# Griffin layer at full precision: six weight panels taken as F32R products of high and low parts, the first normalisation moved behind the products

## What is computed

```
h = rms_norm(x, mix_norm[0])
u = h @ w_in                                  # 1024 -> 2048
gate_branch, x_branch = split(u, 2)
gate_branch = gelu(gate_branch)
xc = causal_depthwise_conv(x_branch, conv_w, conv_b)       # width 4
r = sigmoid(blockwise(xc, w_r) + b_r); i = sigmoid(blockwise(xc, w_i) + b_i)
log_a = 8 * r * log_sigmoid(lam);  a = exp(log_a)
bt = sqrt(-expm1(2 * log_a)) * (i * xc)
h_t = a_t * h_(t-1) + bt_t                    # scan over the 256 tokens
x = x + (gate_branch * h) @ w_out             # 1024 -> 1024
```

## Time and profile before

| | |
|---|---|
| median of 3 runs | 1862.44 us (1861.78 to 1862.58) |
| the profiled execution | 1862.93 us |
| its span, first to last instruction | 1861.7 us |
| PE busy, share of the span | 1739.2 us, 93% |
| DVE, ACT busy | 779.5 us (42%), 584.5 us (31%) |
| mean granted clock of TensorE | 0.983 |
| end of the Griffin layer's last product | 110.8 us from the span's start |

### The profile page before, as it was taken

The page is one execution under the profiler, slowest core; times in us unless marked ns, Lnnn a source line. Parts: engine busy times, 40 slices in busy tenths (PEclk is TensorE's granted clock), DMA queues, the critical chain, the costliest instruction groups (busy, mean ns, idle before and its releaser), DMA issues.

```text
span 1861.7 us, 24238 instructions
## 1 busy us (share of the span) xinstructions
PE 1739.2 (93%) x9217; PEld 1037.3 (56%) x9218; DVE 779.5 (42%) x1132; ACT 584.5 (31%) x758; POOL 30.9 (2%) x56
## 2 busy tenths in 40 slices
PE   6999999988999999998999999999999998999995
PEld 6779997777999898887333332333323232333332
DVE  3544446754444547877322222322222212222224
ACT  1534555544445546653111111211112111111111
POOL 0000001000000020000000000000000000000000
PEclk9999999999999999999899999999999998999998
DMA  7355555421555553347699999999999996999995
GB/s 261 136 181 181 181 182 175 159 74 46 181 181 183 179 186 109 119 148 288 245 431 428 428 428 428 428 428 428 428 429 428 429 398 269 407 428 429 428 428 217
DMA packets 87186, 537.21 MB, mean 289 GB/s; under 512 B 10864, under 2 KB 10968, under 8 KB 62552
## 3 DMA queue, kind: packets, MB, share of 16 engines
q1 hardware_dynamic: 79088, 531.64, 70.9%
q10 hardware_dynamic: 8040, 4.73, 0.9%
HBM read 535.31 MB, written 1.05 MB: 288 GB/s over the span
## 4 chain that ended last, share of the span: by engine, by line
PE 63%; DMA 26%; DVE 6%; ACT 2%; issue 2%; ACTq 0%; SPq 0%; PEldq 0%; POOL 0%; DVEq 0%; POOLq 0%
DMA expert_ring<-in_expert_w_up 26%; PE psA L1951 19%; PE psA L537 12%; PE psB L497 11%; PE psB L520 4%; PE psB L389 3%; PE psA L520 2%; PE psB L508 2%; PE psA L412 1%; DVE w_low L478 1%; PE psA L1957 1%; PE psB L344 1%; PE psB L1339 1%; PE psB L1980 1%; PE psA L984 1%
## 5 line engine op out<-in xcount | busy, mean ns | idle before, releaser
L1951 PE MATMUL psA<-expert_ring,gathered_T 128*64 128x512 f32 x1024 | 456.5, 598 | 31.6 <-DMA expert_ring<-in_expert_w_up 31.6
L1952 PE MATMUL psA<-expert_ring,gathered_T 128*64 128x512 f32 x1024 | 456.5, 598 | 0.0
L478 DVE TENSOR_TENSOR w_low<-panel_ring,w_high 128x1024 fp32r<-128x1024 f32 x220 | 267.4, 1223 | 200.8 <-ACT w_high L471 200.0
L1951 PEld LDWEIGHTS psA<-expert_ring,gathered_T 128*64 128x64 f32 x1024 | 135.1, 137 | 346.6 <-issue 282.1
L471 ACT ACTIVATE w_high<-panel_ring 128x1024 fp32r<-128x1024 f32 x220 | 230.2, 1056 | 268.5 <-PE psA L537 105.5
L1951 PE MATMUL psA<-expert_ring,activated_T 128*64 128x512 f32 x528 | 240.5, 598 | 3.1 <-ACT activated_T L2209 0.9
L1952 PE MATMUL psA<-expert_ring,activated_T 128*64 128x512 f32 x528 | 240.5, 598 | 0.0
L2367 DVE TENSOR_SCALAR normed<-psA 128x512 f32<-128x512 f32 x32 | 22.1, 692 | 394.5 <-PE psA L1952 394.5
L2168 ACT ACTIVATE normed<-normed 128x512 f32<-128x512 f32 x32 | 20.2, 630 | 476.0 <-DVE normed L2367 476.0
L497 PE MATMUL psB<-hT_high,w_high 128*128 128x256 f32 x592 | 167.8, 283 | 0.0
L497 PE MATMUL psB<-hT_low,w_high 128*128 128x256 f32 x592 | 167.5, 283 | 0.0
(11 more groups left out here) (439 smaller groups left out, 2563.6 us busy)
## 6 DMA issues: line engine op xcount, KB each, us to landing
expert_ring<-in_expert_w_up SPq DMA_DIRECT2D x128, 2048.0 KB, 25.4
expert_ring<-in_expert_w_down SPq DMA_DIRECT2D x64, 2048.0 KB, 22.3
panel_ring<-in_mlp_w SPq DMA_DIRECT2D x32, 2048.0 KB, 7.9
panel_ring<-in_w_in SPq DMA_DIRECT2D x11, 2048.0 KB, 8.1
panel_ring<-in_fox_w_in SPq DMA_DIRECT2D x6, 2048.0 KB, 8.1
panel_ring<-in_lru_w_in SPq DMA_DIRECT2D x4, 2048.0 KB, 17.9
panel_ring<-in_lru_w_out SPq DMA_DIRECT2D x2, 2048.0 KB, 8.0
panel_ring<-in_fox_w_out SPq DMA_DIRECT2D x2, 2048.0 KB, 8.3
```

The lines of the kernel that those rows point to most:

```text
L478: V.tensor_tensor(w[1], view, w[0].bitcast(F32), ALU.subtract).then_inc(s.w_low, 1)
L1951: M.matmul(ps[0:SLOTS], lhsT, rhs[0], **flags)
L1952: return M.matmul(ps[SLOTS:P], lhsT, rhs[1], **flags)
```

## The change

The Griffin layer's panels go the way of all the others, and the queues of that layer are written anew.

- Panels 0 to 5 become parts 0 to 23: `high` on ACT, `low` on DVE, three F32R products on PE. `part_of` counts from panel 0.
- x is loaded by SP ahead of everything, each half with its own semaphore. The first panel comes as two halves, six of the small loads are issued by SP between them, and the four loads of the gate weights by SP after panel 1. ACT issues six small loads, after one Sqrt on a scratch tile.
- Raw x is transposed as it lands; only the gains (32 columns) are needed by then. 1/rms is made beside the first products, spread over all partitions by two matmuls with a diagonal (`r_diag`, `r_all`), and multiplied into the products as they are evicted (`pad`, `scale_gate`).
- The convolution goes by pairs of channel groups: ACT does the first tap (`first_tap`), DVE the other three (`taps`).
- The gates use Tanh of half the argument in place of Sigmoid, and c4 times the result plus c4 inside Tanh and Exp (per 128-channel group) in place of a multiplication on DVE. a squared is made on ACT. The polynomial for log_sigmoid(lam) goes from DVE to POOL.
- The gated hidden state is split into high and low as well (`gated_high`, `gated_low`).
- After the Griffin layer only counts in waits change.

```diff
 def weights_sp(k, g):
-    S.wait_ge(s.x_loaded, 16 * TT)
-    S.wait_ge(s.small, 16 * SMALL_LOADS)
+    for tt in range(TT):
+        S.dma_start(k.x[:, tt, :], a["x"][0, tt * P:(tt + 1) * P, :]).then_inc(s.x_loaded[tt], 16)
+    S.dma_start(k.panel(0, KD)[:, :, half[0]], sources[0][0][:, :, half[0]]).then_inc(s.first_half, 16)
+    small_loads_sp(k)
+    S.dma_start(k.panel(0, KD)[:, :, half[1]], sources[0][0][:, :, half[1]]).then_inc(s.panel_in[0], 16)
...
+        if p == 1:
+            griffin_loads_sp(k, g)
 def griffin_pe(k, g):
-    project_T(k, GRIFFIN, k.psB[0])
-    project_T(k, GRIFFIN + 1, k.psB[1])
-    gates(0)
-    M.wait_ge(s.evicted, 1)
-    project_T(k, GRIFFIN + 2, k.psB[0])
-    gates(1)
...
+    gains_pe(k)
+    for tt in range(TT):
+        x_T_pe(k, 0, tt)
+    M.wait_ge(s.h_low, 1)
+    product_T_tile(k, p, 0, up(0, 0), 0)
+    product_T_tile(k, p, 1, up(0, 1), 0)
+    M.wait_ge(s.h_low, 2)
+    product_T_tile(k, p, 0, up(0, 0), 1)
+    product_T_tile(k, p, 1, up(0, 1), 1)
+    columns_pe(k)
+    product_T(k, p, 2, up(0, 2))
+    M.wait_ge(s.r_spread, 2)
+    for tt in range(TT):
+        last = M.matmul(k.psA[:, 0, tt * P:(tt + 1) * P], k.ones[:], g.r_diag[:, tt, :], start=True, stop=True)
+    last.then_inc(s.r_rows, 1)
+    product_T(k, p, 3, up(0, 3))
+    for i in range(4):
+        product_T(k, p + 1, i, up(1, i))
+    gates(0)
+    M.wait_ge(s.padded, 2)
+    for i in range(4):
+        if i == 2:
+            gates(1)
+        product_T(k, p + 2, i, up(2, i))
+    M.wait_ge(s.padded, 4)
+    for i in range(4):
+        product_T(k, p + 3, i, up(3, i))
...
+    M.wait_ge(s.gated_low, 1)
+    for i in range(4):
+        product_out(k, p + 4, i, row(i), i == 0)
+    M.wait_ge(s.gated_low, 2)
+    product_out_tiles(k, p + 5, lambda i: row(4 + i), False, True, {(1, 0): lambda: x_T_pe(k, 1, 0)})
 def griffin_act(k, g):
+    def half_tanh(j, n):
+        A.wait_ge(s.gate_products, 2 * j + n + 1)
...
+            last = A.activation((g.ra, g.ib)[n][:, c, :], (g.r_ps, g.i_ps)[n][:, t, :], ACT.Tanh, scale=0.5,
+                                bias=g.half_b[:, KD * n + c:KD * n + c + 1])
+    def decay(j):
+        for f, to in ((ACT.Tanh, g.th), (ACT.Exp, g.ra)):
+            for c in range(4 * j, 4 * j + 4):
+                last = A.activation(to[:, c, :], g.ra[:, c, :], f, scale=g.c4[:, c:c + 1], bias=g.c4[:, c:c + 1])
...
+    squares_act(k, 0)
+    high_h(k, 0, 0)
+    highs(0, 1)
+    high_h(k, 0, 1)
+    highs(1, 3)
+    root_act(k, 0)
+    highs(3, 4)
+    A.wait_ge(s.cols_ready, 2)
+    A.activation(u, k.col("lam", KD), ACT.Abs).then_inc(*act.step())
+    A.activation(u, u, ACT.Exp, scale=-1.0).then_inc(s.lam, 1)
+    highs(4, 6)
+    first_tap(0)
+    highs(6, 8)
+    first_tap(1)
+    highs(8, 9)
+    first_tap(2)
+    highs(9, 11)
+    first_tap(3)
+    highs(11, 12)
+    half_tanh(0, 0)
+    decay(0)
+    half_tanh(0, 1)
+    highs(12, 13)
+    squares(0)
+    highs(13, 14)
+    root(0)
+    half_tanh(1, 0)
+    highs(14, 15)
+    decay(1)
+    highs(15, 16)
+    half_tanh(1, 1)
+    gelu(0)
+    highs(16, 17)
+    gated_high(0)
+    highs(17, 18)
+    squares(1)
+    highs(18, 19)
+    root(1)
+    highs(19, 20)
+    gelu(1)
+    highs(20, 21)
+    gated_high(1)
+    highs(21, 24)
 def griffin_dve(k, g):
+    gains_dve(k)
+    for tt in range(TT):
+        hT_dve(k, 0, tt, gain)
+    low_h(k, 0, 0)
+    lows(0, 1)
+    low_h(k, 0, 1)
+    lows(1, 2)
+    mean_square_dve(k, 0)
+    lows(2, 3)
+    root_dve(k, 0)
...
+    lows(3, 4)
+    columns_dve(k)
...
+    lows(4, 5)
+    V.wait_ge(s.r_rows, 1)
+    V.tensor_copy(g.r_all[:], k.psA[:, 0, 0:T]).then_inc(*dve.step())
+    pad(0)
+    lows(5, 6)
+    taps(0, 1, 2)
+    lows(6, 7)
+    pad(1)
+    taps(0, 3)
+    lows(7, 8)
+    taps(1, 1, 2)
+    lows(8, 9)
+    taps(1, 3)
+    pad(2)
+    lows(9, 10)
+    taps(2, 1, 2)
+    pad(3)
+    lows(10, 11)
+    taps(2, 3)
+    taps(3, 1, 2, 3)
+    lows(11, 12)
+    inputs(0)
+    lows(12, 13)
+    square_gap(0)
+    lows(13, 14)
+    scaled_inputs(0)
+    scan(0)
+    lows(14, 15)
+    scale_gate(0)
+    lows(15, 16)
+    inputs(1)
+    lows(16, 17)
+    gated(0)
+    gated_low(0)
+    lows(17, 18)
+    square_gap(1)
+    lows(18, 19)
+    scale_gate(1)
+    scaled_inputs(1)
+    lows(19, 20)
+    scan(1)
+    lows(20, 21)
+    gated(1)
+    gated_low(1)
+    lows(21, 24)
```

More of the change, by code:

```diff
@@ L604, in __init__ @@
     def __init__(self, k, c):
-        sb = lambda n, shape: k.sb(n, shape, ctx=c)
+        sb = lambda n, shape, dt=F32: k.sb(n, shape, dt, ctx=c)
         self.gate = sb("gate", [P, KD, T])
+        self.parts = [sb(f"gated_{part}", [P, KD, T], F32R) for part in ("high", "low")]
         self.xpad = sb("x_branch", [P, KD, T + 3])
@@ L618, in griffin_pool, with griffin_part, griffin_loads_sp @@
+def griffin_part(n):
+    return GRIFFIN + n // 4, n % 4, BY_COLUMNS if n < 16 else BY_ROW
+def griffin_loads_sp(k, g):
+    S, s, a = k.nc.sync, k.s, k.a
+    S.wait_ge(s.zeroed, 1)
+    for n, name in enumerate(("lru_w_r", "lru_w_i")):
+        w = a[name][0].rearrange("(c n) d e -> d n c e", n=2)
+        for half in range(2):
+            S.dma_start(g.wri[half * 64:half * 64 + 64, n, :, half * 64:half * 64 + 64],
+                        w[:, half, :, :]).then_inc(s.late, 16)
 def griffin_pool(k, g):
-    G, s = k.nc.gpsimd, k.s
+    G, s, pool = k.nc.gpsimd, k.s, k.pool
+    u, sr, s2, acc, c4 = (g.lam[:, i, :] for i in range(5))
@@ new lines, in griffin_pool @@
+    for odd in (13, 11, 9, 7, 5, 3, 1):
+        G.wait_ge(*pool.last())
+        G.tensor_tensor(acc, acc, s2, ALU.mult).then_inc(*pool.step())
+        G.wait_ge(*pool.last())
+        G.tensor_scalar(acc, acc, 2.0 / odd, None, ALU.add).then_inc(*pool.step())
+    G.wait_ge(*pool.last())
+    G.tensor_tensor(acc, acc, sr, ALU.mult).then_inc(*pool.step())
+    G.tensor_scalar(c4, k.col("lam", KD), 0.0, None, ALU.min).then_inc(*pool.step())
+    G.wait_ge(*pool.last())
+    G.tensor_tensor(c4, c4, acc, ALU.subtract).then_inc(*pool.step())
@@ L624, in griffin_pe @@
+    G.wait_ge(*pool.last())
+    G.tensor_scalar(c4, c4, 4.0, None, ALU.mult).then_inc(s.lam, 1)
 def griffin_pe(k, g):
     M, s = k.nc.tensor, k.s
+    up = lambda p, i: by_four(k.psB[p % 2])[:, i, :]
     def gates(j):
@@ L652, in griffin_act @@
-def griffin_act(k, g):
[L653 to L659, removed]
+    gains_pe(k)
+    for tt in range(TT):
+        x_T_pe(k, 0, tt)
+    p = GRIFFIN
+    M.wait_ge(s.h_low, 1)
@@ L685, in griffin_dve, with lows, pad @@
     V, s, dve = k.nc.vector, k.s, k.dve
-    u, sr, s2, acc, ls = (g.lam[:, i, :] for i in range(5))
-    L = k.col("lam", KD)
-    V.wait_ge(s.lam_exp, 1)
+    u, sr, s2 = (g.lam[:, i, :] for i in range(3))
+    gain = k.col("mix", KD)
+    r_all = lambda n: g.r_all[:].unsqueeze(1).to_broadcast([P, n, T])
+    def lows(n0, n1):
+        for n in range(n0, n1):
+            low(k, *griffin_part(n))
+    def pad(n):
+        j, i = n // 2, 2 * (n % 2)
+        V.wait_ge(s.part_done, part_of(GRIFFIN + j, i + 1) + 1)
+        V.wait_ge(s.zeroed, 2)
+        V.tensor_tensor(g.xpad[:, 2 * n:2 * n + 2, 3:3 + T], by_four(k.psB[j])[:, i:i + 2, :], r_all(2),
+                        ALU.mult).then_inc(s.padded, 1)
@@ new lines, in taps @@
+    def taps(n, *ws):
+        V.wait_ge(s.first_tap, n + 1)
+        V.wait_ge(s.padded, n + 1)
+        for w in ws:
+            if w > 1:
+                V.wait_ge(*dve.last())
+            for t in (2 * n, 2 * n + 1):
+                last = V.scalar_tensor_tensor(g.xc[:, t, :], g.xpad[:, t, w:w + T], k.col("conv_w", 1, 8 * w + t),
+                                              g.xc[:, t, :], ALU.mult, ALU.add)
+                if (w, n % 2, t % 2) == (3, 1, 1):
+                    last.then_inc(s.conv_done, 1)
+                else:
+                    last.then_inc(*dve.step())
@@ new lines, in scaled_inputs, with scan, scale_gate @@
+    def scaled_inputs(j):
+        V.wait_ge(s.mult_done, j + 1)
+        V.wait_ge(*dve.last())
+        V.scalar_tensor_tensor(g.ib[:, h4(j)], g.ib[:, h4(j)], 0.5, g.th[:, h4(j)], ALU.mult, ALU.mult).then_inc(*dve.step())
+    def scan(j):
+        V.wait_ge(*dve.last())
+        for t in range(4 * j, 4 * j + 4):
+            V.tensor_tensor_scan(g.th[:, t, :], g.ra[:, t, :], g.ib[:, t, :], 0.0, ALU.mult, ALU.add).then_inc(*dve.step())
+    def scale_gate(j):
+        V.wait_ge(s.part_done, part_of(GRIFFIN + 2 + j, 3) + 1)
+        V.tensor_tensor(g.gate[:, h4(j)], by_four(k.psB[j]), r_all(4), ALU.mult).then_inc(s.gate_scaled, 1)
@@ new lines, in gated, with gated_low @@
+    def gated(j):
+        V.wait_ge(*dve.last())
+        V.wait_ge(s.gelu_done, j + 1)
+        V.tensor_tensor(g.gate[:, h4(j)], g.gate[:, h4(j)], g.th[:, h4(j)], ALU.mult).then_inc(s.gated_h, 1)
+    def gated_low(j):
+        V.wait_ge(s.gated_h, j + 1)
+        V.wait_ge(s.gated_high, j + 1)
```

(15 more changed lines are left out.)

370 lines of the change are left out of this document (156 added, 214 removed).

## The result

| | before | after |
|---|---|---|
| median of 5 runs | 1862.24 us | 1870.54 us (1867.62 to 1874.68) |
| ratio after to before, 95% interval | | 1.0048 (1.0029 to 1.0067) |
| span of the profiled execution | 1861.7 us | 1866.6 us |
| last product of the Griffin layer ends | 110.8 us | 116.3 us |
| from there to the end of the span | 1750.9 us | 1750.3 us |

The changed kernel is slower by 0.5%, where I had forecast a tenth of a percent less and a range up to 1867.5. In the profiled execution all of the loss is in the Griffin layer: 5.5 us at its end, and nothing behind it.

The account below looks back on a forecast made before the run. PE's chain bounds the Griffin layer: 81.5 us of work against 92.6, an earlier start, the low clock and 11 us of stalls move its end from 110.8 to 109.1, the median from 1862.44 to 1860.8 us; range 1855.5 to 1867.5.

Parts of the forecast that it names:

- With the clock up at 18.5: Griffin layer's start: part 0's first tile costs 5.2 us in place of 2.7; part 1 done at 26.7.
- rival C: Clock falls in the Griffin layer's new stalls: 1.5 to 2.4 us more, total 1862.8 us; chance 0.2.
- Rival A: Griffin layer's start: the low clock costs nothing, 4.3 us faster, total 1856.5 us; chance 0.26.
- A's first case: First products: F32R with 128 tokens is not slowed by the low clock, 0.112 us a matmul.
- Start: Griffin layer's start: PE's first product at 13.5 us, 4.7 us won.
- Prices: Costs per instruction in the Griffin layer, such as 0.47 us for decay on ACT, between 0.39 and 0.49.
- The turn into the MLP: From Griffin layer to MLP: held equal, with high of part 24 waiting until 103.8 us.
- Sums: Griffin layer's added work: PE 81.5 us against 92.6 before, DVE 69 us with 24 handovers from ACT.
- Stalls: PE's waits in the Griffin layer: 2.7 us for i gates, 4.7 and 3.7 for gated_low; 11 us together.
- clock 1.00 until there: Expected sign: granted clock at 1.00 until the Griffin layer's last product at 109 us.
- Rival B: ACT's gates: Tanh and Exp don't share a table, 6.4 us more, total 1867.2 us; chance 0.14.
- The slower side: Whole kernel slower by over 0.2%: Rival B and half the errors of the walk, chance 0.2.

Follow-up runs that it names:

- e2_warm: Changed kernel with 9 and 14 idle float32 matmuls before the first product, token halves kept: 1857.49 us, ratio 0.998 to the kernel before.
- e1: Changed kernel with parts 0 and 1 multiplied for all 256 tokens at once, not in halves: 1856.32 us, ratio 0.9976 to the kernel before.
- e4: Kernel before with 12 idle float32 matmuls before the parameters arrive and 14 before the norm's transposes: 1860.97 us, ratio 0.9996 to the kernel before.
- e8: Changed kernel with part 0 in halves but part 1 multiplied for 256 tokens at once: 1863.01 us (one run), no ratio.
- e9: Changed kernel run again, unchanged: 1868.25 us, ratio 1.0038 to the kernel before.
- e5: e1 with gated(0) ahead of low of part 16 and gated(1) ahead of part 20 in DVE's queue: 1854.42 us, ratio 0.9961 to the kernel before.
- e10: e1 with the edits of e5 and e6 together, no idle matmuls: 1853.23 us, ratio 0.9957 to the kernel before.
- e6: e1 with half_tanh(0, 1) ahead of decay(0) in ACT's queue: 1857.15 us, ratio 0.9972 to the kernel before.

## Why the prediction was wrong, step by step

- **Failed: "With the clock up at 18.5 (17.3 if 3.8 us after the start, 22 if at the old place)".** It came up at 37.9. I had taken the delay of the old start, where plain float32 products raised the clock, for any dense work, and bounded it by places of the old trace alone. I had also taken the clock to be low from the start; it was up from 10.6 and fell at 14.0, after the wait of 3.7 us ahead of the first product, a fall that rival C names for the later stalls only. Parts 0 and 1 were done at 34.1, not 26.7, part 2 at 38.8, not 29.8 by the prediction's prices. Of these 9.0 us the shorter waits took back 4.6 (6.5 in place of 11.1), and the later fall of the clock added about 3, so the last product came at 116.3, not 109.1. e2_warm shows the term alone: with the clock up, the layer ends at 105.0. Rival A gave 104.8 for its second case, that the clock is up when the products begin, and that is what e2_warm makes true. A's first case is out: at the low clock a F32R matmul of 128 tokens takes 0.213 us, nearly doubled, as taken.
- Start: first product at 13.68, said 13.5. Right.
- Prices: `decay` 2.08 / 4 = 0.52 us an instruction, said 0.47, outside the bound of 0.49. Two `decay`s of eight steps make 0.8 us. The turn into the MLP held (116.3 to 129.3, 110.8 to 123.9 before), and PE never waited for POOL's chain. The last 78 + 18 matmuls took 24.9 us where the prices give 21.8; the low clock under the first of them makes the difference.
- Sums: three don't come out as written. The old panels and gates add up to 89.6 us and not 92.6; the 3.0 between them are the slow start of panel 0 and the transposes in the chain. DVE's named terms add up to 58.7 us and not 69, and the trace after has DVE busy for 60.4 us of the first 100. A `decay` has 8 small steps, not 8 + 8; its 4.0 us were right for 8. None of these moved the forecast by itself.
- Stalls: for the i gates 1.8 us (said 2.7), for `gated_low(0)` 4.7 (said 4.7), for `gated_low(1)` none (said 3.7). The last went because rival C came true at the stall before: the clock was 0.50 from 89.1 to 95.9, parts 16 to 19 took longer, and DVE caught up. As said there, a fall in the 4.7 us stall was paid out of the next. The seven table loads by 100 us came as said, but "clock 1.00 until there" did not.
- Rival B, separate tables: did not happen. The Trainium skill, ScalarE: Activation LUTs, "Table sets: the hidden batching unit", puts Tanh and Exp in one set; by that rule there is no load, and the trace after agrees: 0 loads from 58.95 to 66.3.
- The slower side had 0.2, all of it on tables and errors of the walk. The case that came, a low clock that lasts because the new first products don't lift it, was not among the rivals. The Trainium skill, TensorE: Matmul & The Clock Gate, "What's actually happening", says that activity of the PE releases the throttle. Here the granted clock stayed at 0.50 through 20 us of F32R matmuls of 128 columns without a gap between them, and the measurement decides.

## What to carry to other kernels

Look at what form the first dense matmuls have, and at the wait ahead of them. In these runs, where the clock had fallen in that wait, F32R products with 128 moving columns left TensorE at 1.2 GHz as long as they lasted, and a split into halves, made to start 1.5 us sooner (13.7 against 15.2), cost 12 at the layer's end. Wide products from the first on (e1), or idle float32 matmuls while the first loads are on their way and until the products start (e2), each gave it back; idle matmuls that stop before a wait (e4) gave 0.9. A reduction in PE's work is worth only what the other queues' handovers let through: look for the low part that stands ahead of the chain which PE waits for.

## What the runs showed of the hardware that was not expected

- F32R matmuls take nearly the same time with 128 and 256 moving columns at both levels of the clock: 0.112 and 0.120 us at 2.4 GHz, 0.213 and 0.213 at 1.2 GHz (starts in the changed kernel from 14 to 34 us and from 34.4 to 37.8).
- The clock rose 2.3 to 6.0 us after the first F32R product with 256 columns in the seven kernels that met it at the low clock (3.5 in the changed kernel, 3.6 in e8), and not in the 20 us of those with 128 that the changed kernel and its repetition e9 ran. When it was up before them, it stayed up through 96 of them (e2).
- It also rose behind 16 float32 transposes of 128 columns (at 10.6 us in the changed kernel, and so in e5, e8, e9 and e10, though not in e1 and e6) and fell again, at 14.0 in the changed kernel, where PE had waited from 10.0 to 13.7.
- An activation that reads both scale and bias from columns costs 0.52 us on 128x256, start to start, against 0.39 with a bias alone.
